# Half-height matmuls in one projection group: eight chunks of a decoder trunk computed as pairs over the upper and lower 64 rows of the array

## The reference, cut to what matters

```python
h = rms_norm(x, norm_mix_g[i])
z = h @ w_in[i]
z_glu, gq, gk, gv, gr, ga, mq, mk, mv = jnp.split(z, offsets, axis=-1)
y_a = conformer_conv_branch(z_glu, ...)
y_b = gla_branch(gq, gk, gv, gr, ga, ...)
y_c = moba_branch(mq, mk, mv, ...)
gates = jax.nn.sigmoid(h @ w_gate[i] + b_gate[i]).reshape(b_sz, s, N_BRANCH, d)
merged = gates[:, :, 0] * y_a + gates[:, :, 1] * y_b + gates[:, :, 2] * y_c
x = x + merged @ w_out[i]
```

## Time and profile before

| what | value |
|---|---|
| median of three runs | 1588.03 us |
| the profiled execution | 1587.09 us |
| its span, first to last instruction | 1585.1 us |
| PE busy | 1572.8 us, 99% |
| PE weight loads busy | 1328.3 us, 84% |
| DVE, ACT busy | 1044.2 us, 783.6 us |
| granted clock of PE | 1.00 in every slice (2.4 GHz) |
| matmuls | 7834 |

### The profile page before, as it was taken

The page is one execution under the profiler, slowest core; times in us unless marked ns, Lnnn a source line. Parts: engine busy times, 40 slices in busy tenths (PEclk is TensorE's granted clock), DMA queues, the critical chain, the costliest instruction groups (busy, mean ns, idle before and its releaser), DMA issues.

```text
span 1585.1 us, 21519 instructions
## 1 busy us (share of the span) xinstructions
PE 1572.8 (99%) x7834; PEld 1328.3 (84%) x7834; DVE 1044.2 (66%) x1225; ACT 783.6 (49%) x928; POOL 34.4 (2%) x52
## 2 busy tenths in 40 slices
PE   8999999999999999999999999999999999999998
PEld 6888888888888888888888888888888888888887
DVE  5699766665677555655677777764457777765554
ACT  6445554544655444454555555543345555544443
POOL 5000100000000000000000000000000000000000
PEclk9999999999999999999999999999999999999999
DMA  7666655666655666556566666656666566666564
GB/s 258 189 179 178 186 174 171 186 180 179 195 177 178 196 198 194 185 185 186 175 198 180 179 198 194 189 195 191 196 187 188 172 197 186 197 189 191 175 202 146
DMA packets 156227, 297.16 MB, mean 187 GB/s; under 512 B 9575, under 2 KB 12483, under 8 KB 156160
## 3 DMA queue, kind: packets, MB, share of 16 engines
q1 hardware_dynamic: 155648, 296.00, 61.6%
q0 software_dynamic: 480, 0.25, 0.1%
q10 hardware_dynamic: 32, 0.01, 0.0%
HBM read 294.12 MB, written 2.10 MB: 187 GB/s over the span
## 4 chain that ended last, share of the span: by engine, by line
PE 98%; DVE 1%; ACT 0%; issue 0%; DMA 0%; ACTq 0%; DVEq 0%
PE psum L496 21%; PE psum L497 21%; PE psum L498 21%; PE psum L480 20%; PE psum L483 11%; PE psum L615 1%; PE psum L662 0%; PE psum L563 0%; DVE w_lo L1190 0%; PE psum L673 0%; PE psum L523 0%; PE psum L631 0%; PE psum L650 0%; PE psum L547 0%; ACT w_hi L875 0%
## 5 line engine op out<-in xcount | busy, mean ns | idle before, releaser
L1190 DVE TENSOR_TENSOR w_lo<-raw,w_hi 128x1024 fp32r<-128x1024 f32 x549 | 668.9, 1223 | 456.0 <-ACT w_hi L875 455.2
L875 ACT CAST w_hi<-raw 128x1024 fp32r<-128x1024 f32 x549 | 574.5, 1051 | 625.9 <-PE psum L498 477.5
L480 PE MATMUL psum<-h_both,w_hi 128*128 128x512 f32 x1408 | 352.6, 392 | 0.0
L496 PE MATMUL psum<-w_hi,h_both 128*128 128x512 f32 x860 | 340.0, 395 | 0.1
L498 PE MATMUL psum<-w_hi,h_both 128*128 128x512 f32 x860 | 335.0, 390 | 0.0
L497 PE MATMUL psum<-w_lo,h_both 128*128 128x512 f32 x860 | 334.9, 389 | 0.0
L480 PEld LDWEIGHTS psum<-h_both,w_hi 128*128 128x128 f32 x1408 | 253.4, 189 | 45.4
L483 PEld LDWEIGHTS psum<-h_both,w_lo 128*128 128x128 f32 x1408 | 192.1, 190 | 13.7
L483 PE MATMUL psum<-h_both,w_lo 128*128 128x256 f32 x1408 | 196.3, 282 | 0.0
L498 PEld LDWEIGHTS psum<-w_hi,h_both 128*128 128x128 f32 x860 | 161.4, 188 | 34.3
L496 PEld LDWEIGHTS psum<-w_hi,h_both 128*128 128x128 f32 x860 | 161.5, 188 | 33.4 <-DVE h_both L1218 0.6
(11 more groups left out here) (270 smaller groups left out, 1093.0 us busy)
## 6 DMA issues: line engine op xcount, KB each, us to landing
raw<-in_w_up SPq DMA_DIRECT2D x176, 512.0 KB, 3.8
raw<-in_w_gate SPq DMA_DIRECT2D x96, 512.0 KB, 3.7
raw<-in_w_in SPq DMA_DIRECT2D x90, 512.0 KB, 3.6
raw<-in_w_down SPq DMA_DIRECT2D x88, 512.0 KB, 4.5
raw<-in_w_out SPq DMA_DIRECT2D x32, 512.0 KB, 3.8
raw<-in_w_ple_gate SPq DMA_DIRECT2D x32, 512.0 KB, 4.4
raw<-in_w_moba_out SPq DMA_DIRECT2D x16, 512.0 KB, 3.9
raw<-in_w_conv_out SPq DMA_DIRECT2D x8, 512.0 KB, 4.0
```

The source lines that it names most:

```text
L480: nc.tensor.matmul(wide[part][:, j, :], w_hi[:, c % RING, w], h_both[:, kt + k, :, :].rearrange("p h s -> p (h s)"), start=first and k == ...
L496: nc.tensor.matmul(o, sh, w_hi[:, c % RING, w], start=first and k == 0, stop=False, skip_group_check=True)
L875: A.copy(w_hi[:, c % RING, :], raw[:, c % RING, :]).then_inc(chunk_high, 1)
L1190: V.tensor_tensor(w_lo[:, c % RING, :], raw[:, c % RING, :], w_hi[:, c % RING, :].bitcast(F32), ALU.subtract).then_inc(chunk_split, 1)
```

## The change

In the group `mv` 0 alone (chunks 74 to 81) `token_chunk` is replaced by a new routine, `half_chunk`. It has two blocks. In the first, five of the six products of a chunk are done with the upper 64 partitions for one token half and with the lower 64 for the other, alternating matmul by matmul: ten matmuls of 64 rows. Then the sixth product of one token half (`whole`) is done over 128 partitions. In the second block the token halves change places. Before it PE waits for a new semaphore, `halves_swapped`, which the last 64-row matmul of the first block counts up: so an upper and a lower half never write one bank at the same time. From chunk to chunk the order of the token halves is turned round, so that a swap is only needed inside a chunk. A chunk has 20 matmuls of 64 rows and 2 of 128, each still with 128 stationary and 512 moving columns.

```diff
+    halves_swapped = sem("halves_swapped")
...
+        def half_chunk(c, s, j, kt, first, last):
+
+            pe.wait_ge(chunk_split, c + 1)
+            dst = flat(acc[s])
+            upper, lower = slice(0, 64), slice(64, P)
+
+            def terms(t, r):
+                for k in range(2):
+                    w = slice(k * W, (k + 1) * W)
+                    sh, sl = h_hi[r, kt + k, t * P:(t + 1) * P], h_lo[r, kt + k, t * P:(t + 1) * P]
+                    yield k, sh, w_hi[r, c % RING, w]
+                    yield k, sh, w_lo[r, c % RING, w]
+                    if k == 0:
+                        yield k, sl, w_hi[r, c % RING, w]
+
+            def whole(t, stop):
+                return nc.tensor.matmul(dst[:, t * W:(t + 1) * W], h_lo[:, kt + 1, t * P:(t + 1) * P], w_hi[:, c % RING, W:2 * W],
+                                        start=False, stop=stop, skip_group_check=True)
+
+            order = (0, 1) if j % 2 == 0 else (1, 0)
+            for half, turn in enumerate(order):
+                if half:
+                    pe.wait_ge(halves_swapped, j + 1)
+                for i, pair in enumerate(zip(terms(turn, upper), terms(1 - turn, lower))):
+                    for t, (k, stat, mov) in zip((turn, 1 - turn), pair):
+                        mm = nc.tensor.matmul(dst[:, t * W:(t + 1) * W], stat, mov, start=first and half == 0 and i == 0, stop=False,
+                                              skip_group_check=True)
+                if half == 0:
+                    mm.then_inc(halves_swapped, 1)
+                mm = whole(turn, last)
+            mm.then_inc(chunk_used, 1)
...
-                    token_chunk(c, s, h_hi, h_lo, 2 * j, first, last)
+                    if name == "mv" and g == 0:
+                        half_chunk(c, s, j, 2 * j, first, last)
+                    else:
+                        token_chunk(c, s, h_hi, h_lo, 2 * j, first, last)
```

## The result

The changed kernel takes 1593.77 us (median of 7 runs, 1593.54 to 1594.10), the kernel before 1588.03 (1587.40 to 1588.29, 7 runs). The ratio is 1.0038, with a 95% interval of 1.0028 to 1.0048: 5.7 us slower, where 6.0 was forecast and 1594.0 named.

The account below looks back on a forecast made before the run. PE's own work, one matmul after the other, was taken as the bound. Pairs +0.3, height changes +6.15 and the vanished wait -0.5 gave +5.95 us on a 1585.1 span, so 1594.0 us; own range 1592.5 to 1597, whole range 1590 to 1602.

Parts of the forecast that it names:

- PE's time is the kernel's time: Chunks 74 to 81: a microsecond added to PE adds one to the total unless it falls into a wait.
- Two halves in one slot: Chunks 74 to 81: two 64-row matmuls run side by side in one 0.227 us slot; 80 pairs, +0.3 us.
- The surcharge: On each of the 80 pairs, 0.004 us extra because the 0.11 us step read from the levels is rounded: +0.3 us.
- The estimate from the Trainium skill: For the 80 pairs, another price from the skill's page: 1.10 slots a pair, +1.8 us instead of +0.3.
- Changes of height: Between 128-row and 64-row matmuls on PE: holes of 0.41 us for in and out, 15 each, +6.15 us.
- The rival of no holes behind long streams: At the turns between float32r matmuls of 512 columns, a long stream hides drain and load: 1587.8 us, chance 10%.
- How many: Eight chunks, 16 blocks: 15 new ways in and 15 out, level 1 into chunk 80 free; otherwise 16, +6.6 us.
- The semaphore: PE's eight waits for `halves_swapped`: signal there 0.27 us early, no cost; uncovered rival up to +3.8 us, chance 5%.
- The idle time before level 1: PE's 0.48 us wait for DVE after chunk 79 goes, because PE then comes last: -0.5 us.
- the two waits that I named as slack: ACT and DVE wait for PE in this stretch, 1.66 and 1.70 us, so nothing becomes late.
- The range: Forecast's own range for the kernel's time: holes 5.4 to 7.5, pairs 0 to 1.1, 1 for misses, -0.5: 1592.5 to 1597 us.

Follow-up runs that it names:

- no full matmuls at all: Against the changed kernel, all six products of a block are 64-row pairs, with the swap wait directly behind the last pair: 1590.05 us, ratio 1.0015.
- both groups: Against the changed kernel, the same routine also in the second mv group, so for chunks 74 to 89: 1600.1 us, ratio 1.0075.
- the halves apart: Against the changed kernel, each block does its five upper 64-row matmuls first, then its five lower ones: 1599.31 us, ratio 1.0070.
- Laid open: Against the changed kernel, each block begins with its 128-row matmul, so the swap wait stands directly behind the last pair: 1594.76 us, ratio 1.0042.
- twelve and twelve: Against the changed kernel, two chunks as one, blocks of twelve upper then twelve lower matmuls, no 128-row ones, one swap per two chunks: 1604.2 us, ratio 1.0103.

## Why the prediction was right, step by step

1. **PE's time is the kernel's time.** The stretch of the group grew by 5.98 us and the median of the runs by 5.7; nothing behind the group gave any back (0.13 us more in the profiled execution).
2. **Two halves in one slot.** Right for float32r and 512 columns too, though only 64- and 128-column float32 halves were to be seen before. Away from holes a pair is 0.227 us. The surcharge that I had put on it (+0.3) belongs to the slots just behind a hole: a block is 1.79 us with one pair as with five, 0.43 above six slots, and I had 0.41 for the holes and 5 x 0.004 for the pairs. One term was too small by what the other had too much, and that they cancel is luck; where the pairs were as many and the holes fewer, or the other way round, it shows (no full matmuls at all: 0.4 too much for the pairs; both groups: 0.3 too little for the holes). The estimate from the Trainium skill ("TensorE: Matmul & The Clock Gate", "Part 3: Packing small matmuls"), 1.10 slots for a pair, isn't borne out by the undisturbed pairs of the run without full matmuls, which take 1.00. The same section's 4 ns for a second tile fits the starts (the second matmul of a pair starts 0 to 23 ns behind the first in the changed kernel, 4 in the median), not the period.
3. **Changes of height.** 0.31 to 0.33 in, 0.33 out, 0.33 to 0.34 with an exposed load, as read from the levels. The same pieces came out with one pair or five between them, and with 8 instead of 15 each way 2.7 of 5.7 us went. It is the height and not the pairing: with the halves apart a single half-height matmul stands behind the full one, and full to half is 0.44 (230.65 to 231.09 in that run), as in front of a pair. The rival of no holes behind long streams had its own conditions here, and failed.
4. **How many.** I counted 15 each way, with the way from level 1 into chunk 80 free. It has no drain (0.07 us between starts), but its load is still exposed: 0.31 to the next pair instead of 0.23. So 0.08 us of that way is left, the only part of the count that was off. The rule that a change of tiling mode drains, and one of tile does not (the Trainium skill, "TensorEngine Tiling (Array Packing)", "Key Properties"), agrees: 0.33 where the height changes, 0.07 where only the kind of work does.
5. **The semaphore.** Covered: from the full matmul to the next pair it is 0.42 with the wait (230.18 to 230.60) and 0.44 in front of the next chunk, where this wait isn't (231.97 to 232.41). Laid open, the waiting matmul starts 0.45 to 0.46 behind the one that counts the semaphore up (I had taken 0.48, from ACT). That costs 0.13 where the height changes anyway, and behind a pair 0.23, with the exposed weight load 0.34.
6. **The idle time before level 1** went, as computed. Of the two waits that I named as slack, only ACT's is for PE; DVE's 1.70 us are for ACT, which comes to the same.
7. **The range.** Its upper end follows from its terms (7.5 + 1.1 + 1 - 0.5 = 9.1, 1597.1 us); the lower one should have been 5.4 - 1 - 0.5 = 3.9, 1591.9 us and not 1592.5. The measured time is inside either way.

What stays open: which part of a hole is the drain itself and which the start of the load could not be separated further, and that the second stream is the lower half is read from the operands' order, since the rows give no half for a single matmul.

## What to carry to other kernels

Splitting a full-height matmul into two half-height ones wins nothing: the pair takes the slot that the full one took. In this kernel each change between full and half height cost 0.2 us on the way in and 0.2 on the way out, 0.43 together, so count the changes, and keep work of one height together (two changes a chunk instead of four brought back nearly half of the loss). Where 64-row matmuls are the nature of the work, write upper and lower ones alternately: five and five in a row cost 0.35 us a block, twelve and twelve cost 16 us in the whole group, where the pairs with full matmuls between them cost 5.7.

## What the runs showed of the hardware that was not expected

The two halves of the array do not take their matmuls strictly in program order: the first matmul of the other half starts beside one that stands four places ahead of it, the second of five and the ninth of twelve, and overtakes the three between. The Trainium skill says the opposite ("TensorE: Matmul & The Clock Gate", "Part 3": matmuls start and end in program order); the order of `w_hi` and `w_lo` among the measured starts and the 5.5 us instead of 14.5 decide it for these runs. It would also mean that a semaphore counted up by the last matmul of one half says less about the other half than its place in the program suggests. No run shows such a case; here the last one written was the last to start in each block shown.
